# Norm's mean from its rows, opening by row tiles, modulation in quarters, and the values ahead of the root in head 0

## The chip, the cores and the metric

The kernel runs on one core of a Trainium2 chip. The time is device microseconds of one execution. TensorE multiplies (PE in the profile, with its weight loads PEld), VectorE (DVE) and ScalarE (ACT) do the elementwise work, GpSimd (POOL) and SyncE (SP) here mostly issue DMAs. All engines run on their own and meet at semaphores.

## The reference

One step of a two layer diffusion backbone on 128 context and 512 latent tokens (640 columns in five row tiles), 1024 channels. Layer 0 mixes by latent attention with 8 heads, layer 1 by a Conformer convolution; each is followed by a SwiGLU FFN. Each part starts from a root mean square norm with a shift and a scale that a conditioning vector makes:

```python
sh1, sc1, g1, ... = split(silu(cond) @ w_mod[l] + b_mod[l], 6)
h = rms_norm(x, norm_mix[l]) * (1 + sc1) + sh1
# layer 0
q = rms_norm((rms_norm(h @ w_dq) @ w_uq) per head);  kv = h @ w_dkv
k, v = split(rms_norm(kv[:256]) @ w_ukv);  k = rms_norm(concat(k, kv[256:]))
o = softmax(q k^T * scale) v
# layer 1
y = depthwise_conv(glu(h @ w_pw1))
y = silu((y - mean(y)) * rsqrt(mean((y - mean(y))**2) + eps) * ln_g + ln_b) @ w_pw2
```

## The kernel before

The program is written by hand for each engine: every engine has its list of instructions and waits for semaphores. Activations lie with channels on the partitions (eight tiles of 128 channels, `KT`) and tokens along the row. Precision comes from three products for each matmul: a number is split in a high and a low part (`HH` and `HL`, `WH` and `WL`), and `split3` adds high x high, high x low and low x high. PSUM is used as four tiles of two banks, given out in the order of `tile_order()`: the n-th name gets tile n mod 4, and `begin` waits until the tile's last user was read. `filled` waits for a product, `was_read` for the release of its tile.

*Opening.* SyncE loads x (`XROWS`, by rows), the first weights (`RAW`, unit `dkv` 0) and the first 2048 columns of `w_mod`, as two halves of 512 columns of shift and scale each, in 8 loads per half (`MODS`). TensorE turns x into channel order (L805), sums its squares over the channels (L817), and multiplies the modulation's rows (L853), four column groups of 32 at once; ScalarE copies the rows (`MROW`), TensorE turns them (L864), VectorE adds the bias and makes the gains (`first_half`, L1814 and L1819). The sums are turned too (L829), VectorE takes their inverse root and makes diagonals, which TensorE spreads over the partitions (`spread`, L790) and ScalarE copies to `RSTD`. Then `apply` makes, tile by tile, the scaled tile (L1891, VectorE), its high part (L1330, ScalarE) and its low part (L1905, VectorE), and TensorE runs the pair `dkv` 0 and 1 over the eight tiles k0 to k7. Half the modulation's columns serve tiles 0 to 3, the other half tiles 4 to 7; the second half's rows are multiplied inside the pair (`second_half`). `hold_clock` multiplies constants, to keep TensorE at work.

*Head 0.* Keys, queries and values come from the same unit. TensorE turns the values (`v`, L1006), ScalarE copies their high part `VH` and VectorE makes the low part `VL` (L2104). The head's squares are summed to `hsum`, copied to `HROW` (L1463), turned (`hst`), and VectorE makes the root and six diagonals (L2093); their spread is `rk`. The order of tiles is `v`, `hsum`, `hst`, `s` 0, `rk`, so `rk` gets the tile of `v`.

*LayerNorm.* The convolution's eight tiles `Y` are shifted by an estimate of their mean (`SHIFT`), tiles 0 to 5 by DMAs of GpSimd; ScalarE squares them (`LNQ`, L1709), and TensorE sums the squares (L1235) and the tiles (`srow`). The rest of the mean is spread over the partitions by matmuls with ones (`mean_part`, L1242), and leaves as `OFFSET`. ScalarE then makes a low part for a later unit (L1674), loads the table of Silu (L1716) and copies `RSTD`.

## Time and profile before

| | |
|---|---|
| median of 3 runs | 1640.55 us (1639.95 to 1641.98) |
| the profiled run | 1642.74 us, its span 1640.9 us |
| TensorE busy | 1607.8 us, 98% |
| VectorE, ScalarE, GpSimd busy | 56%, 41%, 18% |
| the DMAs | 178.12 MB, mean 109 GB/s |
| mean granted clock of TensorE | 0.993 |

The busy share of TensorE is an average; what counts for a change in one place is which wait ends last there. So the timeline and the waits of that place are read, with the granted clock beside them (1.0 is 2.4 GHz, 0.5 is 1.2 GHz).

### The profile page before, as it was taken

What the parts mean: (1) busy time and instruction counts of PE and PEld (TensorE: products, weight loads), DVE (VectorE), ACT (ScalarE), POOL (GpSimd) and SP (SyncE); (2) the same over time, 40 slices, a digit from 0 to 9 for tenths busy, and PEclk for the clock granted to TensorE, in tenths of its full rate; (3) what the DMA queues carried; (4) which work ended last, traced back from release to release, by engine and by line L of the source; (5) the groups of instructions that cost most, each with busy time, mean ns of one, the idle gap of its engine ahead of it and who ended that gap; (6) DMA issues with size and microseconds to landing.
All of it is one profiled execution on the core that took longest, in us unless ns stands there. A gap on an engine that the chain in (4) does not pass through costs nothing.

```text
span 1640.9 us, 26141 instructions
## 1 busy us (share of the span) xinstructions
PE 1607.8 (98%) x11077; PEld 1558.9 (95%) x11077; DVE 922.3 (56%) x1537; ACT 666.4 (41%) x1002; POOL 287.6 (18%) x344
## 2 busy tenths in 40 slices
PE   7989999999999999999999999999999999999998
PEld 5889889899999999999999999989999999999998
DVE  4646667665776645455367889987742323223232
ACT  3435555553544323342335656674432212221121
POOL 0011111000155423453342022230000000000000
PEclk8999999999999999999999999999999999999999
DMA  9322333132254433443333288873232122222211
GB/s 320 99 66 84 92 99 103 35 116 78 89 162 141 155 112 122 155 133 123 115 115 108 55 180 180 182 138 98 71 94 78 61 77 77 77 77 77 71 59 65
DMA packets 140157, 178.12 MB, mean 109 GB/s; under 512 B 12769, under 2 KB 116905, under 8 KB 139016
## 3 DMA queue, kind: packets, MB, share of 16 engines
q1 hardware_dynamic: 117824, 109.68, 21.0%
q0 software_dynamic: 21888, 66.66, 16.2%
q8 instruction: 88, 1.44, 0.4%
q14 instruction: 29, 0.24, 0.0%
q10 hardware_dynamic: 328, 0.10, 0.0%
HBM read 148.93 MB, written 2.79 MB: 92 GB/s over the span
## 4 chain that ended last, share of the span: by engine, by line
PE 85%; DVE 10%; DMA 2%; ACT 2%; issue 1%; POOL 0%; SPq 0%; DVEq 0%; ACTq 0%; POOLq 0%
PE PS L693 26%; PE PS L695 25%; PE PS L698 25%; DVE YACC L2319 6%; DMA ZACC<-ZTAP 1%; PE PS L763 1%; PE PS L1019 1%; PE PS L790 1%; PE PS L1030 1%; PE PS L982 1%; DMA XROWS<-in_x_sample 1%; DVE GP L2283 0%; PE PS L805 0%; DVE HL L1905 0%; PE PS L963 0%
## 5 line engine op out<-in xcount | busy, mean ns | idle before, releaser
L693 PE MATMUL PS<-HH,WH 128*128 128x320 f32 x1776 | 411.1, 313 | 6.0 <-DVE HL L1905 5.6
L695 PE MATMUL PS<-HL,WH 128*128 128x320 f32 x1776 | 405.5, 310 | 0.0
L698 PE MATMUL PS<-HH,WL 128*128 128x320 f32 x1776 | 404.2, 309 | 0.0
L1756 DVE TENSOR_TENSOR WL<-RAW,WH 128x2048 fp32r<-128x2048 f32 (+2 forms) x87 | 196.4, 2258 | 203.2 <-ACT WH L1294 203.1
L693 PEld LDWEIGHTS PS<-HH,WH 128*128 128x128 f32 x1776 | 295.9, 189 | 10.3 <-issue 6.8
L695 PEld LDWEIGHTS PS<-HL,WH 128*128 128x128 f32 x1776 | 298.6, 189 | 0.0
L698 PEld LDWEIGHTS PS<-HH,WL 128*128 128x128 f32 x1776 | 298.3, 189 | 0.0
L1294 ACT ACTIVATE WH<-RAW 128x2048 fp32r<-128x2048 f32 (+2 forms) x95 | 171.6, 1806 | 111.2 <-PE PS L698 111.2
L1921 DVE SCALAR_TENSOR_TENSOR X<-PS,MODV,X 128x128 f32<-128x128 f32 (+2 forms) x192 | 72.4, 433 | 198.7 <-PE PS L698 198.5
L615 POOL TENSOR_TENSOR BGACC<-BGACC,BGW 128x512 f32<-128x512 f32 x98 | 135.0, 1378 | 194.9 <-ACT BGW L1550 193.8
L693 PE MATMUL PS<-HIDH,WH 128*128 128x320 f32 x704 | 162.3, 312 | 0.7 <-DVE HIDL L2242 0.7
L698 PE MATMUL PS<-HIDH,WL 128*128 128x320 f32 x704 | 160.7, 309 | 0.0
L695 PE MATMUL PS<-HIDL,WH 128*128 128x320 f32 x704 | 160.5, 309 | 0.0
L1550 ACT ACTIVATE BGW<-BGW,SC 128x512 f32<-128x512 f32 x112 | 80.7, 723 | 157.4 <-DVE BGACC L1859 116.4
L2319 DVE SCALAR_TENSOR_TENSOR YACC<-GP,WTAP,YACC 128x655 f32<-128x655 f32 x143 | 128.9, 901 | 5.0
L693 PEld LDWEIGHTS PS<-HIDH,WH 128*128 128x128 f32 x704 | 117.0, 188 | 1.3 <-DVE HIDL L2242 0.9
L698 PEld LDWEIGHTS PS<-HIDH,WL 128*128 128x128 f32 x704 | 117.7, 188 | 0.0
L695 PEld LDWEIGHTS PS<-HIDL,WH 128*128 128x128 f32 x704 | 117.5, 188 | 0.0
L2235 DVE TENSOR_TENSOR TMP<-PS,ACTV 128x640 f32<-128x640 f32 x44 | 36.2, 824 | 133.8 <-PE PS L698 132.8
L1585 ACT ACTIVATE HIDH<-TMP 128x640 fp32r<-128x640 f32 x44 | 32.6, 740 | 181.2 <-DVE TMP L2235 181.2
L1859 DVE SCALAR_TENSOR_TENSOR BGACC<-BGW,SC,BGACC 128x512 f32<-128x512 f32 x98 | 86.4, 882 | 4.8
L1580 ACT ACTIVATE ACTV<-PS 128x640 f32<-128x640 f32 x40 | 28.1, 703 | 130.9 <-PE PS L698 130.9
(340 smaller groups left out, 2285.5 us busy)
## 6 DMA issues: line engine op xcount, KB each, us to landing
BGW<-in_w_mod POOLq DMA_DIRECT2D x112, 256.0 KB, 3.0
RAW<-in_ffn_w_gate SPq DMA_DIRECT2D x22, 1024.0 KB, 5.3
RAW<-in_ffn_w_up SPq DMA_DIRECT2D x22, 1024.0 KB, 5.3
RAW<-in_ffn_w_down SPq DMA_DIRECT2D x16, 1024.0 KB, 5.1
MODA<-in_w_mod POOLq DMA_DIRECT2D x48, 256.0 KB, 3.9
MODS<-in_w_mod SPq DMA_DIRECT2D x16, 512.0 KB, 12.3
RAW<-in_conv_w_pw SPq DMA_DIRECT2D x16, 512.0 KB, 5.1
WL<-RAW POOLq DMA_DIRECT2D x8, 1024.0 KB, 10.1
```

Source lines behind the costliest of these rows:

```text
L615: ins = nc.gpsimd.tensor_tensor(acc, acc, w, ALU.add)
L693: mm(o, wh, xh, start=first, stop=False)
L695: mm(o, wh, xl, start=False, stop=False)
L698: ins = mm(o, wl, xh, start=False, stop=last)
L1294: A(WH[:, u % 2, 0:n], RAW[:, u % 2, 0:n], ACT.Copy).then_inc(hi_done, 1)
L1550: A(w, w, ACT.Copy, scale=SC[:, i % KT, 1:2]).then_inc(sem("bgw_scaled"), 1)
L1585: A(HIDH[:, (a + j) % HID_SLOTS, :], TMP[j][:], ACT.Copy).then_inc(sem("hid_hi"), 1)
L1756: V.tensor_tensor(WL[:, u % 2, 0:n], RAW[:, u % 2, 0:n], WH[:, u % 2, 0:n].bitcast(F32), ALU.subtract).then_inc(lo_done, 1)
L1859: ins = V.scalar_tensor_tensor(out=acc, in0=w, scalar=c, in1=acc, op0=ALU.mult, op1=ALU.add)
L1921: ins = V.scalar_tensor_tensor(out=X[:, m, t:t + b - a], in0=tile2(n)[:, bank, a:b], scalar=g, in1=X[:, m, t:t + b - a], op0=ALU.mult, op1 ...
L2235: V.tensor_tensor(row2(TMP[j][:]), tile2(n)[:, :, 0:HALF], row2(ACTV[j][:]), ALU.mult).then_inc(free_of(n), 1)
L2319: ins = V.scalar_tensor_tensor(out=acc[:], in0=g[:, j:j + RUN], scalar=WTAP[:, i, j:j + 1], in1=ZACC[i % 2][:] if i and j == j0 else acc[: ...
```

## The change

*Opening.* x comes in five loads, one for each row tile, and is turned, copied, squared and summed by row tiles. The sums have 640 columns (`MIXROW`) and are turned in five. The first half of the modulation is loaded in front of the first weights; the second half is loaded, multiplied, copied, turned and read in two quarters of 256 columns. The spread of the root stands in front of the turn of the first half. VectorE's first low part of weights stands behind its first scaled tile, and ScalarE's second copy of them behind its first high part. Four groups of held matmuls are gone.

*Head 0.* On ScalarE `values(0)` stands in front of `sum_rows(0)`, on VectorE in front of `head_norm(0)`.

*LayerNorm.* The mean is spread by two matmuls over the turned sums' rows (`LNROW`), with columns of ones where a row belongs to it (`PAIRS`), behind the transposes; `mean_part` is gone. Tile 6 is squared first. The table is loaded in front of `OFFSET`.

```diff
...
-    o = [("x", k) for k in range(KT)] + ["vec"]
-    o += [("stat", "mix0"), ("turn", "mix0"), ("mrow", 0), ("mods", 0), ("rb", "mix0"), ("mrow", 1), ("mods", 1)]
+    o = [("x", t) for t in range(QT)] + ["vec"]
+    o += [("stat", "mix0"), ("turn", "mix0"), ("mrow", 0), ("rb", "mix0"), ("mods", 0), ("mrow", 1), ("mods", 1)]
...
-    o += ["mu", ("srow", "ln"), ("stat", "ln"), ("turn", "ln"), ("rb", "ln")] + [("pw2", m) for m in range(KT)] + ffn(1)
+    o += [("srow", "ln"), ("stat", "ln"), ("turn", "ln"), "mu", ("rb", "ln")] + [("pw2", m) for m in range(KT)] + ffn(1)
...
-        XSQ = [*SQ, *TMP, *ACTV, SUM, RSTD]
+        XSQ = [sb(f"XSQ{t}", [P, KT, P], R_T[0] + 4096 * t) for t in range(QT)]
+        MIXROW = sb("MIXROW", [P, TOK], R_T[0])
...
-            def load_mods(h):
+            def load_mods(h, part, c0, n):
                 for k in range(KT):
                     w = w_mod[0, k * P:(k + 1) * P, 0:2 * D].rearrange("p (c n) -> p c n", c=2)
-                    sp.dma_start(MODS[h][k][:], w[:, :, h * 512:(h + 1) * 512]).then_inc(mods_landed[h][k], 16)
+                    c = 512 * h + c0
+                    sp.dma_start(MODS[h][k][:, :, c0:c0 + n], w[:, :, c:c + n]).then_inc(mods_landed[part][k], 16)
...
-            sp.dma_start(XROWS[:, 0, :], x_prompt[0]).then_inc(sem("x_landed"), 16)
-            sp.dma_start(XROWS[:, 1:QT, :], x_sample[0].rearrange("(t p) d -> p t d", p=P)).then_inc(sem("x_landed"), 16)
+            sp.dma_start(XROWS[:, 0, :], x_prompt[0]).then_inc(x_landed[0], 16)
+            for t in range(1, QT):
+                sp.dma_start(XROWS[:, t, :], x_sample[0, (t - 1) * P:t * P, :]).then_inc(x_landed[t], 16)
+            load_mods(0, 0, 0, 512)
...
-                    load_mods(0)
-                    load_mods(1)
+                    load_mods(1, 1, 0, 256)
+                    load_mods(1, 2, 256, 256)
...
+            for t in range(QT):
+                ps = begin(("x", t))
+                if t == 0:
                     hold_clock(ps, HOLD)
-                    pe.wait_ge(sem("x_landed"), 32)
-                for t in range(QT):
-                    ins = tr(flat(ps)[:, t * P:(t + 1) * P], XROWS[:, t, k * P:(k + 1) * P], EYE[:])
+                pe.wait_ge(x_landed[t], 16)
+                for k in range(KT):
+                    ins = tr(flat(ps)[:, k * P:(k + 1) * P], XROWS[:, t, k * P:(k + 1) * P], EYE[:])
...
+            for t in range(QT):
+                pe.wait_ge(sem("sq_made"), SQ_BASE["mix0"] + t + 1)
+                for e in range(2):
+                    for g in range(GROUPS):
+                        ins = mm(ps[COLG * g:COLG * (g + 1), t // 4, t % 4 * P:(t % 4 + 1) * P], ONES[:, 0:COLG], XSQ[t][:, 2 * g + e, :],
+                                 start=(e == 0), stop=(e == 1))
+            ins.then_inc(mm_done, 1)
             def turn_sums():
-                hold_clock(ps, HOLD // 4)
                 out = begin(("turn", "mix0"))
                 was_read(pe, ("stat", "mix0"))
-                for i in range(3):
-                    ins = tr(out[:, 0, i * P:(i + 1) * P], HROW[:, i * P:(i + 1) * P], EYE[:])
+                for t in range(QT):
+                    ins = tr(flat(out)[:, t * P:(t + 1) * P], MIXROW[:, t * P:(t + 1) * P], EYE[:])
                 ins.then_inc(mm_done, 1)
-                hold_clock(out, HOLD // 4)
...
+            def later_rows(q):
+                rows = begin(("mrow", 1)) if q == 0 else tile2(("mrow", 1))
+                for k in range(0, KT, 2):
+                    pe.wait_ge(mods_landed[1 + q][k], 16)
+                    pe.wait_ge(mods_landed[1 + q][k + 1], 16)
+                    for g in range(GROUPS):
+                        i = k + g // 2
+                        ins = mm(rows[COLG * g:COLG * (g + 1), q, 0:256], SC[:, i, :], MODS[1][i][:, g % 2, 256 * q:256 * (q + 1)],
+                                 start=(k == 0), stop=(k == KT - 2))
+                ins.then_inc(mm_done if q else sem("part_rows"), 1)
...
+            def turn_later(q):
+                if q == 0:
+                    pe.wait_ge(sem("part_copied"), 1)
+                    turn_rows_of(begin(("mods", 1)), 0, range(2)).then_inc(sem("part_turned"), 1)
+                else:
+                    was_read(pe, ("mrow", 1))
+                    turn_rows_of(tile2(("mods", 1)), 1, range(2, 4)).then_inc(mm_done, 1)
             def second_half(k, j):
                 if (k, j) == (0, 1):
-                    first_rows(1, KT // 2, KT - 2)
-                if (k, j) == (2, 0):
-                    first_rows(1, KT - 2, KT)
-                if (k, j) == (2, 1):
-                    turn_first(1)
+                    later_rows(0)
+                if (k, j) == (3, 1):
+                    later_rows(1)
+            turn_sums()
             pe.wait_ge(sem("sc_ready"), 2)
-            first_rows(0, 0, KT // 2)
-            turn_sums()
-            first_rows(0, KT // 2, KT)
-            turn_first(0)
+            first_rows()
             spread(("rb", "mix0"), diagn, DIAGS["mix0"])
-            first_rows(1, 0, KT // 2)
+            turn_first()
...
+                if k == KT // 2 - 1:
+                    turn_later(0)
                 if k == KT // 2:
+                    turn_later(1)
...
+                    pe.wait_ge(sem("sq_made"), SQ_BASE["ln"] + k + 3)
...
-            mean_part(SEVENS, SHIFT, True, False)
             pe.wait_ge(sem("sq_added"), NORMS["mu"])
-            mean_part(ONES, SUM, False, False).then_inc(mm_done, 1)
             for g in range(GROUPS):
                 mm(means[COLG * g:COLG * (g + 1), 0, 0:3 * P], (ONES, SEVENS)[g // 2][:, 0:COLG], (SUM, SHIFT)[g // 2][:, halves3[g % 2]],
                    start=True, stop=g >= 2)
-            for k in range(0, KT - 2, 2):
-                square_sums(k)
+            square_sums(0)
+            square_sums(2)
             pe.wait_ge(sem("last_shifted"), 1)
             for g in range(2):
                 ins = mm(means[COLG * g:COLG * (g + 1), 0, 0:3 * P], ONES[:, 0:COLG], Y[:, KT - 1, halves3[g]], start=False, stop=True)
             ins.then_inc(mm_done, 1)
+            square_sums(4)
...
-            mean_part(ONES, Y[:, KT - 1, :], False, True).then_inc(sem("mean_whole"), 1)
+            mean = begin("mu")
+            pe.wait_ge(sem("pairs_made"), 2)
+            for i in range(2):
+                ins = mm(mean[:, i, 0:HALF], PAIRS[i][:], LNROW[:, 1, i * COLG * 2:i * COLG * 2 + HALF], start=True, stop=True)
+            ins.then_inc(mm_done, 1)
...
+            for t in range(QT):
+                was_read(act, ("x", t))
+                A(XSQ[t][:], X[:, :, t * P:(t + 1) * P], ACT.Square).then_inc(sem("sq_made"), 1)
...
-            A(HROW[:], tile2(("stat", "mix0"))[:, 0, 0:3 * P], ACT.Copy).then_inc(free_of(("stat", "mix0")), 1)
+            A(MIXROW[:], flat(tile2(("stat", "mix0")))[:, 0:TOK], ACT.Copy).then_inc(free_of(("stat", "mix0")), 1)
+            filled(act, ("mrow", 0))
+            A(MROW[:], tile2(("mrow", 0))[:, 0, :], ACT.Copy).then_inc(free_of(("mrow", 0)), 1)
+            spread_copy(("rb", "mix0"), RSTD, QT)
             act.wait_ge(raw_landed[0], landed[0])
             A(WH[:, 0, 0:UNIT // 2], RAW[:, 0, 0:UNIT // 2], ACT.Copy).then_inc(sem("hi_first"), 1)
-            A(WH[:, 0, UNIT // 2:UNIT], RAW[:, 0, UNIT // 2:UNIT], ACT.Copy).then_inc(hi_done, 1)
-            n_hi[0] += 1
-            def first_row_copy(h):
-                filled(act, ("mrow", h))
-                A(MROW[:], tile2(("mrow", h))[:, 0, :], ACT.Copy).then_inc(free_of(("mrow", h)), 1)
-            first_row_copy(0)
-            spread_copy(("rb", "mix0"), RSTD, QT)
             def first_between(k):
-                if k == KT // 2 - 1:
-                    first_row_copy(1)
+                if k == 0:
+                    A(WH[:, 0, UNIT // 2:UNIT], RAW[:, 0, UNIT // 2:UNIT], ACT.Copy).then_inc(hi_done, 1)
+                    n_hi[0] += 1
+                if k == 2:
+                    act.wait_ge(sem("part_rows"), 1)
+                    A(MROW[:, 0:256], tile2(("mrow", 1))[:, 0, 0:256], ACT.Copy).then_inc(sem("part_copied"), 1)
+                if k == 3:
+                    filled(act, ("mrow", 1))
+                    A(MROW[:, 256:512], tile2(("mrow", 1))[:, 1, 0:256], ACT.Copy).then_inc(free_of(("mrow", 1)), 1)
...
+            values(0)
             sum_rows(0)
-            values(0)
             spread_copy(("rk", 0), RK, NKT)
             for h in range(HEADS):
                 for t in range(QT):
...
                 if i:
                     tap_diagonals(i)
                     conv_out(i - 1)
-            for i in range(KT - 1):
+            for i in (KT - 2, *range(KT - 2)):
                 act.wait_ge(y_shifted[i], 16)
                 A(LNQ[i][:], Y[:, i, :], ACT.Square).then_inc(sem("sq_made"), 1)
             for b, n in ((1, ("srow", "ln")), (0, ("stat", "ln"))):
                 filled(act, n)
                 A(LNROW[:, b, :], tile2(n)[:, 0, 0:3 * P], ACT.Copy).then_inc(free_of(n), 1)
-            act.wait_ge(sem("mean_whole"), 1)
+            A(REC8[:, 0:1], ONES[:, 0:1], ACT.Silu)
...
-            A(LNSS[:, 0:1], ONES[:, 0:1], ACT.Silu)
...
+                if first is not None:
+                    first()
...
+                V.tensor_copy(X[:, :, t * P:(t + 1) * P], flat(tile2(n)).rearrange("p (k c) -> p k c", c=P)).then_inc(free_of(n), 1)
...
-            dve.wait_ge(sem("hi_first"), 1)
-            split_first(0)
-            n_lo[0] += 1
+            def low_first():
+                dve.wait_ge(sem("hi_first"), 1)
+                split_first(0)
+                n_lo[0] += 1
...
-                    first_half(1)
-            first_half(0)
-            apply("mix0", 0, 0, second=between)
+                    dve.wait_ge(sem("part_turned"), 1)
+                    first_part(("mods", 1), 0, 4, 6)
+                if k == KT // 2:
+                    filled(dve, ("mods", 1))
+                    first_part(("mods", 1), 1, 6, 8)
+            filled(dve, ("mods", 0))
+            first_part(("mods", 0), 0, 0, 4)
+            apply("mix0", 0, 0, second=between, first=low_first)
...
             queries(0)
+            values(0)
             head_norm(0)
-            values(0)
             split_units(U[("head", 1)])
             for h in range(HEADS):
                 was_read(dve, ("rk", h))
...
             for s in range(2):
                 link(V.tensor_tensor(GB[:, s, :], MODV[:, 1, s, 16:24], VT2[:, V2["b_pw2"]:V2["b_pw2"] + KT], ALU.mult))
+            for g in range(2):
...
+                rows = EYE[:].rearrange("p (e g c) -> p g c e", e=2, g=2)[:, g, 0:1, :]
+                link(V.tensor_reduce(out=LNSS[:, g:g + 1], in_=rows, op=ALU.add, axis=mybir.AxisListType.X))
+                V.tensor_scalar(PAIRS[g][:], ONES[:], LNSS[:, g:g + 1], None, ALU.mult).then_inc(sem("pairs_made"), 1)
...
```

TensorE in the opening, from the last rows of the first half (`MODS_6`, `MODS_7`) to the first product of the pair (`HH`, `WH`); before:

```order
L853 MATMUL PS<-MODS_6_63,SC 32x512 [waits mods_landed0_7,mods_landed0_6]
L853 MATMUL PS<-MODS_6_63,SC 32x512
L853 MATMUL PS<-MODS_7_64,SC 32x512 x2
L864 MATMUL PS<-PICK_185,MROW 128x4 [waits tile_read3,pick_made,tile_read0]
L864 MATMUL PS<-PICK_185,MROW 128x4 x3
L790 MATMUL PS<-DIAGN,ONES 128x128 [waits diag_ready,tile_read1]
L790 MATMUL PS<-DIAGN,ONES 128x128 [waits diag_ready] x4
L853 MATMUL PS<-MODS_0_65,SC 32x512 [waits mods_landed1_1,mods_landed1_0,tile_read2]
...
L693 MATMUL PS<-HH,WH 128x320 [waits lo_first,h_ready,tile_read1,tile_read0]
```
and now:

```order
L853 MATMUL PS<-MODS_6_63,SC 32x512 [waits mods_landed0_7,mods_landed0_6]
L853 MATMUL PS<-MODS_6_63,SC 32x512
L853 MATMUL PS<-MODS_7_64,SC 32x512 x2
L796 MATMUL PS<-DIAGN,ONES 128x128 [waits diag_ready,tile_read1]
L796 MATMUL PS<-DIAGN,ONES 128x128 [waits diag_ready] x4
L872 MATMUL PS<-PICK_193,MROW 128x4 [waits tile_read0,pick_made,tile_read2]
L872 MATMUL PS<-PICK_193,MROW 128x4 x3
L699 MATMUL PS<-HH,WH 128x320 [waits lo_first,h_ready,tile_read2,tile_read1]
```
The spread (`DIAGN`) moved in front of the turn (`PICK`), and the rows of the second half left the place in front of the pair.

ScalarE inside the pair, from the high part of tile 3 to that of tile 4 (`HH`), with the copy of the modulation's rows (`MROW`); before:

```order
L1330 ACTIVATE HH<-SQ_87,MODV 128x128 [waits t_ready]
L1330 ACTIVATE HH<-SQ_87,MODV 128x512
L1330 ACTIVATE HH<-TMP_89,MODV 128x128 [waits t_ready]
L1330 ACTIVATE HH<-TMP_89,MODV 128x512
L1382 ACTIVATE MROW<-PS 128x512 [waits mm_done]
L1330 ACTIVATE HH<-TMP_90,MODV 128x128 [waits t_ready]
L1330 ACTIVATE HH<-TMP_90,MODV 128x512
```
and now:

```order
L1349 ACTIVATE HH<-SQ_87,MODV 128x128 [waits t_ready]
L1349 ACTIVATE HH<-SQ_87,MODV 128x512
L1406 ACTIVATE MROW<-PS 128x256 [waits part_rows]
L1349 ACTIVATE HH<-TMP_89,MODV 128x128 [waits t_ready]
L1349 ACTIVATE HH<-TMP_89,MODV 128x512
L1409 ACTIVATE MROW<-PS 128x256 [waits mm_done]
L1349 ACTIVATE HH<-TMP_90,MODV 128x128 [waits t_ready]
L1349 ACTIVATE HH<-TMP_90,MODV 128x512
```
One copy became two, the first of them in front of tile 3.

VectorE in head 0, around the root (`RS`) and its diagonals (`DIAGK`); before:

```order
L2040 SCALAR_TENSOR_TENSOR QNL<-PS,GQK,QNH 128x640 [waits qn_hi]
L2088 TENSOR_TENSOR HST<-PS,KPSS 128x12 [waits mm_done]
L2090 SCALAR_TENSOR_TENSOR RS<-HST,MODV 128x12 [waits tile_read1]
...
L2093 TENSOR_SCALAR DIAGK_137<-EYE,RS 128x128 [waits dve_chain]
...
L2094 TENSOR_SCALAR RQ_193<-RS 128x6
L2104 TENSOR_TENSOR VL<-PS,VH 128x768 [waits v_hi,dve_chain]
L1756 TENSOR_TENSOR WL<-RAW,WH 128x1024 [waits hi_done]
```
and now:

```order
L2071 SCALAR_TENSOR_TENSOR QNL<-PS,GQK,QNH 128x640 [waits qn_hi]
L2135 TENSOR_TENSOR VL<-PS,VH 128x768 [waits v_hi]
L2119 TENSOR_TENSOR HST<-PS,KPSS 128x12 [waits mm_done]
L2121 SCALAR_TENSOR_TENSOR RS<-HST,MODV 128x12 [waits tile_read2]
...
L2124 TENSOR_SCALAR DIAGK_143<-EYE,RS 128x128 [waits dve_chain]
...
L2125 TENSOR_SCALAR RQ_201<-RS 128x6
L1775 TENSOR_TENSOR WL<-RAW,WH 128x1024 [waits hi_done,dve_chain]
```
`VL` moved from behind the diagonals to in front of the sums.

## Rows read from the trace of the kernel before

**Rows 1.** The page, part 4: shares of the chain that ended last.
```profile
PE 85%; DVE 10%; DMA 2%; ACT 2%; issue 1%; POOL 0%; SPq 0%; DVEq 0%; ACTq 0%; POOLq 0%
```

**Rows 2.** Timeline of PE, opening (start, us, line, out<-in, count, idle before it and its releaser).
```profile
10.87 7.39 PE L805 MATMUL PS<-EYE,XROWS 128*128 128x128 f32 x40 [3.55 <-DMA XROWS<-in_x_sample]
...
24.06 1.92 PE L853 MATMUL PS<-MODS,SC 128*32 128x512 f32 x16
...
30.51 1.03 PE L864 MATMUL PS<-PICK,MROW 128*128 128x4 f32 x8 [0.81 <-ACT MROW L1382]
31.39 1.36 PE L790 MATMUL PS<-DIAGN,ONES 128*128 128x128 f32 x10
...
36.94 0.70 PE L693 MATMUL PS<-HH,WH 128*128 128x320 f32 x2 [2.34 <-DVE HL L1905]
...
51.03 0.53 PE L693 MATMUL PS<-HH,WH 128*128 128x320 f32 x2 [2.04 <-DVE HL L1905]
...
58.34 0.68 PE L838 MATMUL PS<-EYE,TAPROWS 31*128 31x31 f32 x8
```

**Rows 3.** Loads of the tile MODS, one issued between 13.2 and 13.9 us at the latest.
```profile
L535 SPq DMA_DIRECT2D MODS<-in_w_mod x1: 1300/1300/1300, 13.1 to 13.1; - x1
...
DMA to landing us min/median/max: 12.4/12.4/12.4
```

**Rows 4.** Windows: busy time of PE, PEld, DVE, ACT, POOL, then clock, DMA share, GB/s.
```profile
11.00:13.00 2.00, 2.00 (x10) 2.00 (x11) 0.77 (x1) 0.00 (x0) 0.00 (x0) 0.50 1.08 354
22.00:30.00 8.00, 7.70 (x67) 3.77 (x63) 2.37 (x15) 2.61 (x4) 0.00 (x0) 1.00 1.05 388
37.20:40.50 3.30, 3.30 (x16) 2.91 (x19) 3.30 (x7) 1.91 (x4) 0.00 (x0) 0.50 0.29 82
119.10:125.80 6.70, 4.48 (x19) 4.48 (x20) 3.72 (x12) 0.95 (x2) 0.00 (x0) 0.50 0.26 81
```

**Rows 5.** Timeline of DVE, opening.
```profile
30.36 1.22 DVE L1947 TENSOR_TENSOR WL<-RAW,WH 128x1024 fp32r<-128x1024 f32 x1
31.57 0.24 DVE L1814 TENSOR_TENSOR MODV<-PS,VT 128x8 f32<-128x8 f32 x2
...
33.62 1.94 DVE L1891 SCALAR_TENSOR_TENSOR TMP<-X,GAIN,RSTD 128x128 f32<-128x128 f32 x4 [1.54 <-ACT RSTD L1307]
```

**Rows 6.** Timeline of ACT, opening.
```profile
29.77 0.60 ACT L1382 ACTIVATE MROW<-PS 128x512 f32<-128x512 f32 x1 [3.83 <-PE PS L853]
```

**Rows 7.** Timeline of PE, head 0.
```profile
118.24 0.27 PE L1019 MATMUL PS<-KPL,QP 128*128 128x128 f32 x1
121.32 2.93 PE L790 MATMUL PS<-DIAGK,ONES 128*128 128x128 f32 x12 [2.81 <-DVE VL L2104]
```

**Rows 8.** Timeline of DVE, head 0.
```profile
116.88 0.17 DVE L2088 TENSOR_TENSOR HST<-PS,KPSS 128x12 f32<-128x12 f32 x1 [1.35 <-PE PS L971]
...
118.93 1.27 DVE L2093 TENSOR_SCALAR DIAGK<-EYE,RS 128x128 f32<-128x128 f32 x6
...
120.31 0.96 DVE L2104 TENSOR_TENSOR VL<-PS,VH 128x768 fp32r<-128x768 f32 x1
```

**Rows 9.** Timeline of ACT, head 0.
```profile
115.69 0.49 ACT L1463 ACTIVATE HROW<-PS 128x384 f32<-128x384 f32 x1 [1.08 <-PE PS L963]
116.07 0.81 ACT L1477 ACTIVATE VH<-PS 128x768 fp32r<-128x768 f32 x1
```

**Rows 10.** Timeline of PE, LayerNorm.
```profile
1091.91 2.12 PE L1235 MATMUL PS<-LNQ,ONES 128*32 128x384 f32 x24
...
1096.32 1.24 PE L1242 MATMUL PS<-Y,ONES 128*128 128x320 f32 x4
...
1100.07 1.28 PE L790 MATMUL PS<-DIAGN,ONES 128*128 128x128 f32 x10
```

**Rows 11.** Timeline of ACT, LayerNorm.
```profile
1091.70 1.36 ACT L1709 ACTIVATE LNQ<-Y 128x640 f32<-128x640 f32 x2 [0.92 <-DMA Y<-SHIFT]
...
1100.12 1.28 ACT L1716 ACT_TABLE_LOAD   x1
```

94 lines of the change are left out of this document (39 added, 55 removed).

## The prediction

> **What bounds the kernel now.** I read the page's chain of waits first. TensorE carries 85% of the chain that ended last, VectorE 10% [rows 1], so the kernel is a nearly closed row of matmuls, and time is to be had only where that row is open. Every part of the change lies in one of three such places: the opening, head 0, and the LayerNorm of the convolution. For each I read the timeline of the three engines, and asked what ends each wait of TensorE last.
>
> *Opening.* The transposes of x begin at 10.87, when the one load of the four latent row tiles lands, and end at 18.2; the modulation's rows run until their copy at 29.77 [rows 6], its turn at 30.51, the spread of the root at 31.39, and the first product of the layer starts at 36.94, after 2.34 us of waiting for VectorE. The second half of the modulation's columns is interleaved with that pair of products, which stands once more at 51.03 for 2.04 us and is over at 58.34 [rows 2]. The loads are full work: 388 GB/s from 22 to 30 us, and 354 GB/s while the first weights come in packets of 1 KB [rows 4]. The eighth load of modulation was issued at 13.1 and landed 12.4 us later, at 25.5 [rows 3].
>
> *Head 0.* The root's six diagonals are made from 118.93, but the spread starts at 121.32 and waited 2.81 us for VL, the values' low part, which VectorE makes only at 120.31 [rows 7, 8]: `rk` uses the PSUM tile that `v` held. TensorE's clock is at half from 119.1 to 125.8 [rows 4].
>
> *LayerNorm.* TensorE works through without a gap, but on too much: the sums of squares start at 1091.91 behind four 320 column products, the last piece of the mean at 1096.32, and the spread at 1100.07 [rows 10]. ScalarE loads its table at 1100.12, on the path [rows 11].
>
> **The opening, step by step.** The x tiles now arrive one by one and are copied in five pieces of 1024 columns instead of eight of 640 (VectorE), squared likewise, and summed per row tile. From about 8.5, my guess for when the first tile is turned, five copies at 1.2 (as WL of 1024 columns [rows 5]), a square of as much, the sums and their copy make about 17 us; that has 5 us to spare and isn't the path. What stands last is the modulation. Now its first half (8 loads of 0.52 MB) follows x directly, and the 1 MB of weights comes behind it. From 10.8: 8 x 0.524 MB at 388 GB/s is 10.8 us, so 21.6. The same sum for the kernel before (1.05 MB at 354 GB/s first, 3.0 us) gives 24.6, and it landed at 25.5; I keep that 0.9, so 22.5. Then TensorE: the last two tiles of rows are half of 1.92 (four tiles), to 23.5; the spread 1.3, to 24.8; the turn 1.0, to 25.9, with the copies of 0.60 and the like beside it [rows 2, 6]. VectorE: reading 0.24 + 0.23, to 26.4; then two scaled tiles of about 0.95, WL (now behind the first scaled tile) 1.2, and one low part of 0.95 [rows 5], to 30.5. First product at 30.6 instead of 36.94. The weights' first half must be there by 27.4 for this: landed 25.5, and a copy of 1024 columns is at most 1.2, so 26.7. SyncE issues the same bytes; the 16 loads of quarters have 256 KB each, and `dkv` 2 and the late loads stand behind them as before.
>
> Not all of those 6.3 us stay, because the second half's rows are now all inside the pair. One k step is (58.34 - 51.03) / 4 = 1.8 us at full clock. Before, the first was at half clock, as from 37.2 to 40.5 [rows 4], and cost 3.4. I assume the same now, since TensorE stands idle from 25.9 to 30.6. So: k0 3.4, first quarter's rows 1.9 (as many columns as four half tiles), k1 and k2 3.6, turn 0.5, k3 1.8, second quarter's rows 1.9: 13.1, to 43.7. These rows now lie behind k3, and ScalarE waits for them with its copy **before** the high part of tile 4, so everything queues: copy about 0.45, high part 0.95, low part 0.95, gaps 0.1: k4 at 46.2. VectorE next reads the last gains (0.5), scales and takes the low part of tile 5 (1.9): k5 at 48.6, k6 at 50.5, k7 at 52.3, end of the pair at 54.05 instead of 58.34. **Opening: -4.3 us.** The quarters' loads land, at 354 GB/s (0.524 MB x 4 = 2.1 MB, 5.9 us each), at 31.4 and 37.3, ahead of their use at 34.0 and 41.8; the late loads are queued behind them as before. Bounds: if the clock is full from 30.6 on, 1.6 more is won (-5.9); if it falls already between 22.5 and 26, the spread, rows and turn take about twice as long and the start slips by 2.2 (-2.1). I take the middle, since the kernel before shows one fall here.
>
> One rule speaks against this part. Loads of 512 KB moved 388 GB/s from 22 to 30 us, one in 1.35 us, and the eighth was 12.4 us under way, so about nine overlap [rows 3, 4]; the sum above goes by that. The Trainium skill, "DMA: Bandwidth & Descriptors", section Bandwidth, asks for loads of 1 MiB or more to reach 75% of peak, and gives each load some 2 us of fixed cost. An estimate by its fit, without overlap, is 2.6 us for 256 KB, quarters at 46 and 67 us and a kernel slower than before. The trace disagrees with that at 512 KB, and no run here shows 256 KB; a milder form is a rival below.
>
> **Head 0.** Both moves fill holes. On ScalarE VH (0.81) now precedes HROW, which had 1.08 us of idle time before it [rows 9]; on VectorE VL (0.96) precedes the sums, before which it had 1.35 idle [rows 8]. So neither delays the root: the sums are read at 116.88 as before, and the first diagonal is there at 119.15, when the scores of the context are over (118.5, the last product of rows 7 started 118.24). What is late next is the root itself. Spread: 12 instructions, at full clock 1.55 (ten took 1.28 in the LayerNorm [rows 10]), to 120.7 instead of 121.32 + 2.93 = 124.25: 3.55. Before, TensorE ran at half until 125.8, which cost another 0.8. **Head 0: -4.3 us** if the clock doesn't fall. If it falls at 119 and rises at 122.5, the spread takes 2.9 and the first scores are slowed: -2.8.
>
> **LayerNorm.** Ahead of the squares' sums, 8 matmul instructions of 320 columns go (1.24 us twice, as in the row of 1096.32), and the last piece behind the transposes goes too; two products of 320 columns over the turned row take their place (1.1). The squares now end with tile 5, whose DMA decides: ScalarE's two last squares ran 1091.70 to 1093.06, so tile 5 is squared at 1092.4; TensorE has done the others, and sums 2 x 0.65, to 1093.75. Before, 24 of these instructions ended at 1094.0, and 0.63 for the mean of tile 7 and 0.65 for tiles 6 and 7 made it 1095.3. Everything behind is 1.6 earlier: turn, root, mean (over at 1095.95 instead of 1097.57), held clock, spread over at 1099.7. ScalarE has loaded its table (1.28 + 0.2) while it waited for the mean, and starts the spread's copy at 1099.8 instead of 1101.6, to where the table held it [rows 11]. The new VectorE instructions (two reductions, two of 128x128, about 1 us) fall where it waits for the turned sums. **LayerNorm: -1.7 us**, bounds -1.4 and -2.2. Late next: TensorE's own held clock in front of the spread.
>
> **Sum:** -4.3 - 4.3 - 1.7 = -10.3 us. The profiled run took 1642.74 us (span 1640.9), so its like would be 1632.4; the median of the three runs is 2.2 lower, and gives 1640.55 - 10.3 = 1630.2. Behind the pair TensorE hardly waits until head 0, and all loads there are released by compute, so I let the gain pass.
>
> **Rivals.**
> *The clock falls in the wrong places* (2 in 10). Held matmuls are removed between 18 and 28 us, and TensorE has more gaps there. For it: half clock stands in rows 4 behind each long gap. Against: the modulation's rows are work too. Opening -2.1, head 0 -2.8, LayerNorm -1.7: 1634.0. In the Trainium skill, "TensorE: Matmul & The Clock Gate", Part 1, the throttled state is the default and activity releases it; what is removed here is such activity, and the traces agree that the clock falls behind gaps.
> *The clock holds in the opening* (1.3 in 10): -5.9 - 4.3 - 1.7: 1628.7.
> *Small loads are slow* (0.6 in 10): if a 256 KB load takes as long as one of 512 KB (1.35 us), the quarters land at 36.3 and 47.1; the second rows end 4 us later, the opening gives 0.3, sum 6.3: 1634.3. Against: the 1 KB packets of the weights at 354 GB/s.
> *The change doesn't do what it says in head 0* (0.4 in 10): something else, say QP's moves, holds the spread as long: 1634.5. Against: the scores in front of it were over at 118.5 [rows 7].
> *Slower* (0.3 in 10): the clock stays at half from the spread at 23.5 to the end of the pair. Price: 1.3 + 1.0 of spread and turn, 14.4 of k steps, 3.8 of rows, 1.0 of turns is 21.5 us of work that would take twice as long, less the 1.6 counted and some 3 that hide in waits: +17, so 1647. It decides for slower once the half clock there is over 20 us longer than counted. Against: both falls of rows 4 ended while TensorE worked.
>
> **Numbers.** Forecast 5.4 in 10. Range 1627 to 1635: it takes in all cases but the last and the edges. About 0.2% (3.3 us) is what a measurement of this kernel can tell: faster 0.93, same 0.04, slower 0.03.
>
> **What would show it.** First product of the layer at about 30.6, pair over at 54; a wait of TensorE for low part 4 in front of k4; the spread of head 0 started by 119.3 and waiting for diagonals; the LayerNorm's spread over 1.6 us sooner after the end of the convolution, and ScalarE's copy waiting for TensorE. Wrong if the eighth modulation load lands after 24, if the quarters land later than 34 and 42, or if the gain is lost to half clock.

## The result: 5.8 us faster where 10.3 were forecast

| | before | after |
|---|---|---|
| median of 15 runs | 1641.76 us (1639.24 to 1644.20) | 1636.00 us (1632.11 to 1639.13) |
| ratio | | 0.9968 (0.9960 to 0.9976) |
| profiled run, its span | 1642.74, 1640.9 us | 1635.48, 1633.7 us |

The sign was right, the size was not: 1636.0 lies above the range of 1627 to 1635. The two profiles differ by 7.2 us, but 1.4 of that is an end of the profiled run of before that no other one has: from the last transpose to the end of the span it took 6.7 us, in the thirteen other profiles of this study 5.2 to 5.3. Until then after is 5.83 us ahead, which is what the medians say too. The starts of the same work, one trace against the other:

| place | before | after | gain so far | forecast |
|---|---|---|---|---|
| first product | 36.94 | 30.41 | 6.53 | 6.3 |
| pair over | 58.34 | 54.22 | 4.12 | 4.3 |
| values' transposes, head 0 | 113.02 | 108.90 | 4.12 | 4.3 |
| `kn` 1, behind head 0's scores | 130.75 | 124.11 | 6.64 | 8.6 |
| last matmul of the convolution | 1088.85 | 1083.03 | 5.82 | 8.6 |
| first product behind the LayerNorm | 1105.76 | 1099.93 | 5.83 | 10.3 |

So three terms fell short: head 0 by 1.8 us, the way from there to the convolution's end by 0.8, the LayerNorm by 1.7. The rows of after that answer to [rows 2] (timeline of PE, opening: start, us, line, out<-in, count, idle before it and its releaser):

```profile
7.42 4.63 PE L811 MATMUL PS<-EYE,XROWS 128*128 128x128 f32 x40
...
22.52 1.06 PE L853 MATMUL PS<-MODS,SC 128*32 128x512 f32 x8 [1.65 <-DMA MODS<-in_w_mod]
23.52 1.38 PE L796 MATMUL PS<-DIAGN,ONES 128*128 128x128 f32 x10
...
30.41 0.87 PE L699 MATMUL PS<-HH,WH 128*128 128x320 f32 x2 [4.72 <-DVE HL L1930]
...
46.38 0.53 PE L699 MATMUL PS<-HH,WH 128*128 128x320 f32 x2 [1.50 <-DVE HL L1930]
...
54.22 0.68 PE L840 MATMUL PS<-EYE,TAPROWS 31*128 31x31 f32 x8
```

The eighth load of the modulation ends TensorE's wait at 22.52 (22.5 in the forecast), k4 waits for low part 4 until 46.38 (46.2), and the pair is over at 54.22 (54.05). Head 0, against [rows 7]:

```profile
115.24 2.06 PE L796 MATMUL PS<-DIAGK,ONES 128*128 128x128 f32 x12 [0.88 <-DVE DIAGK L2124]
...
124.11 0.51 PE L699 MATMUL PS<-CKH,WH 128*128 128x384 f32 x2
```

The spread no longer waits for VL but for the diagonals, as foreseen. It takes 2.06 us, not 1.55, because the clock falls inside it. Windows of after (us, busy time of PE, PEld, DVE, ACT, POOL, granted clock, DMA share, GB/s):

```profile
27.60:34.20 6.60, 3.79 (x16) 3.37 (x20) 6.37 (x13) 3.71 (x7) 0.00 (x0) 0.50 1.10 348
116.40:119.50 3.10, 3.10 (x14) 3.10 (x13) 1.48 (x4) 1.40 (x3) 0.00 (x0) 0.50 0.23 53
```

The first row holds the loads of the quarters, 256 KB each: 348 GB/s, so small loads are not slow, and that rival falls; TensorE didn't wait for either quarter (rows multiplied from 33.88 and 41.83, forecast 34.0 and 41.8). The Trainium skill, "DMA: Bandwidth & Descriptors", section Bandwidth, asks for 1 MiB or more per load to reach 75% of peak; this trace shows no such need for loads that overlap like these (512 KB moved 388 GB/s). The 2 us of fixed cost that the prediction puts under the same section stand in the Trainium skill under "Anatomy of one DMA" on that page, for loads that GpSimd issues; these were issued by SyncE. The LayerNorm of after, PE and then ACT, against [rows 10, 11]:

```profile
1085.46 0.85 PE L1257 MATMUL PS<-LNQ,ONES 128*32 128x384 f32 x8 [0.69 <-ACT LNQ L1728]
...
1088.11 1.50 PE L1257 MATMUL PS<-LNQ,ONES 128*32 128x384 f32 x16 [1.17 <-ACT LNQ L1728]
...
1094.36 1.28 PE L796 MATMUL PS<-DIAGN,ONES 128*128 128x128 f32 x10
```
```profile
1084.67 0.74 ACT L1728 ACTIVATE LNQ<-Y 128x640 f32<-128x640 f32 x1 [3.01 <-DMA Y<-SHIFT]
1085.75 0.74 ACT L1728 ACTIVATE LNQ<-Y 128x640 f32<-128x640 f32 x1 [0.34 <-DMA Y<-SHIFT]
1087.33 0.74 ACT L1728 ACTIVATE LNQ<-Y 128x640 f32<-128x640 f32 x1 [0.83 <-DMA Y<-SHIFT]
...
1090.18 1.28 ACT L1732 ACT_TABLE_LOAD   x1
```

All edits are there: no early mean, the table ahead of `OFFSET`. But TensorE, which had no gap here in before, now stands twice for the squares, and ScalarE for 3.01 us for tile 3, whose DMA landed late. From the issue of the first shift's DMA (1079.21 in before, 1073.41 in after) to the square of tile 5, the last that a DMA shifts, it is 12.49 us in before (1091.70) and 13.92 in after. TensorE's gain of 1.4 went into that wait. The six DMAs of the shifts, each from its own issue to its landing (before, then after):

```profile
DMA to landing us min/median/max: 3.7/6.9/9.8
```
```profile
DMA to landing us min/median/max: 3.7/8.0/11.2
```

Counted from the first issue, they land at 3.71, 5.51, 7.42, 9.16, 10.82 and 12.47 us in before, and at 3.70, 5.55, 7.50, 11.24, 12.32 and 13.89 in after: the first three are on time, the fourth is 2.1 late.

Why did the DMAs take longer? A window of after at their end; then the queues' packets, MB and share from the first shift's DMA to the last one's end (1073.4 to 1087); then, from the page, parts 1 and 3, the counts of the whole run:

```profile
1085.60:1086.90 1.30, 1.30 (x12) 0.25 (x7) 1.20 (x5) 0.74 (x1) 0.00 (x0) 1.00 0.06 12
```
```profile
q0 software_dynamic: 969, 2.20, 92.2%
q8 instruction: 1, 0.02, 0.4%
```
```profile
PE 1599.7 (98%) x11123; PEld 1553.6 (95%) x11123; DVE 922.9 (56%) x1541; ACT 666.2 (41%) x1000; POOL 287.6 (18%) x344
...
q8 instruction: 88, 1.44, 0.4%
```

A DMA share of 0.06 over 1.3 us is one engine of sixteen. The packets, sampled every 0.25 us, say the same: from 7 to 11.75 us behind the first issue 16 to 20 of them are in flight, and from 12.25 to 13.5 us exactly one, where before has none. The queue of instructions moved 88 packets in 1.44 MB, so 16 KB each, for 22246 instructions of TensorE (matmuls and weight loads), about 253 a packet. They are TensorE's: between one packet and the next lie 255 to 258 of its instructions in the median, in all fourteen traces. The one of these fetches in the second fence started at 1082.57, 9.2 us behind the first shift's DMA, when the fourth DMA was next to land. In before they lay 4.0 us ahead of it and 17.2 behind. That made theory F (the texts below call it theory A): the change adds about 112 instructions of TensorE ahead of the convolution (14938 of them stand ahead of the first shift's DMA, 14825 in before), so each fetch comes at an earlier place in the program. One now falls among the shifts' DMAs, where it holds up one of the sixteen engines that each of them needs.

### The profile page after: what moved, and what is told of

It is laid out like the page before. It is cut to its first block, busy times and chain, and to the rows that moved or that the text cites. A ratio compares the mean times of both kernels' runs of the same rounds, so it can differ in the third digit from the quotient of the medians.

```text
span 1633.7 us, 26252 instructions
## 1 busy us (share of the span) xinstructions
PE 1599.7 (98%) x11123; PEld 1553.6 (95%) x11123; DVE 922.9 (56%) x1541; ACT 666.2 (41%) x1000; POOL 287.6 (18%) x344
## 3 DMA queue, kind: packets, MB, share of 16 engines
q0 software_dynamic: 21888, 66.66, 16.4%
q8 instruction: 88, 1.44, 0.4%
## 4 chain that ended last, share of the span: by engine, by line
PE 83%; DVE 9%; DMA 4%; ACT 2%; issue 1%; SPq 1%; POOL 0%; DVEq 0%; ACTq 0%; POOLq 0%
PE PS L699 26%; PE PS L701 25%; PE PS L704 25%; DVE YACC L2350 4%; DMA ZACC<-ZTAP 2%; PE PS L769 1%; PE PS L1041 1%; PE PS L796 1%; PE PS L1052 1%; DMA MODS<-in_w_mod 1%; DMA Y<-SHIFT 1%; PE PS L1004 1%; DVE GP L2314 0%; DVE HL L1930 0%; PE PS L985 0%
```

## The experiments

Twelve runs, one of them after again. Medians, with those of the kernel before from the same comparison:

| | us | before | ratio |
|---|---|---|---|
| e1 LayerNorm alone | 1638.94 | 1641.14 | 0.9991 (0.9982 to 1.0000) |
| e2 head 0 alone | 1637.60 | 1641.14 | 0.9982 (0.9972 to 0.9992) |
| e3 after, held opening | 1633.78 | 1641.14 | 0.9954 (0.9942 to 0.9966) |
| e4 after, both held | 1630.22 | 1641.14 | 0.9935 (0.9923 to 0.9947) |
| e5 opening alone | 1639.37 | 1641.41 | 0.9985 (0.9976 to 0.9993) |
| e6 after again | 1634.46 | 1641.41 | 0.9955 (0.9943 to 0.9968) |
| e7 e4, fetch back | 1640.51 | 1641.41 | 0.9990 (0.9982 to 0.9999) |
| e8 e4, rows early | 1629.45 | 1641.41 | 0.9924 (0.9912 to 0.9936) |
| e9 after, fetch away | 1639.94 | 1640.67 | 0.9992 (0.9983 to 1.0000) |
| e10 before, fetch into | 1647.67 | 1640.67 | 1.0039 (1.0026 to 1.0051) |
| e11 e4, old head 0 | 1634.31 | 1640.67 | 0.9955 (0.9943 to 0.9967) |
| e12 e8, last head held | 1627.50 | 1640.67 | 0.9917 (0.9904 to 0.9930) |

What their traces show, in the second table. *Pair*: when the pair is over; for e7, e9 and e10 less the work inserted behind it. *Head 0*: from the values' transposes to `kn` 1, with the half clock in it. *Fetch*: those next to the first shift's DMA, from its issue. *Tile 5*: from that issue to its square. *LN*: from the last convolution matmul to the first product behind the LayerNorm.

| | pair | head 0 | half clock | fetch | tile 5 | LN |
|---|---|---|---|---|---|---|
| before | 58.34 | 17.73 | 6.8 | -4.0, +17.2 | 12.49 | 16.91 |
| e1 | 55.74 | 17.65 | 6.8 | -3.9, +16.6 | 12.50 | 15.49 |
| e2 | 57.26 | 15.04 | 3.4 | -4.0, +17.2 | 12.50 | 16.91 |
| e10 | 57.5 | 18.13 | 6.8 | **+9.7** | 13.67 | 17.42 |
| e5 | 54.27 | 18.41 | 6.8 | **+9.1** | 13.86 | 17.65 |
| after | 54.22 | 15.21 | 3.4 | **+9.2** | 13.92 | 16.90 |
| e6 | 54.19 | 15.19 | 3.4 | **+8.5** | 13.44 | 16.46 |
| e9 | 55.7 | 13.64 | 0 | -4.3, +16.4 | 12.49 | 15.48 |
| e3 | 53.51 | 16.12 | 6.8 | +0.4, +19.5 | 12.49 | 15.48 |
| e4 | 52.50 | 13.62 | 0 | -3.5, +16.5 | 12.50 | 15.48 |
| e7 | 52.4 | 14.01 | 0 | **+11.9** | 14.28 | 18.55 |
| e8 | 50.54 | 13.62 | 0 | -3.5, +16.5 | 12.48 | 15.53 |
| e11 | 53.52 | 17.12 | 3.4 | -4.1, +14.3 | 12.48 | 15.47 |
| e12 | 51.09 | 13.63 | 0 | -5.2, +14.5 | 12.48 | 14.69 |

**e1, the LayerNorm alone.** The hunks of `mu`, `mean_part`, `PAIRS`, the order of the squares and the table, on the kernel before:

```diff
-            mean_part(SEVENS, SHIFT, True, False)
...
+                ins = mm(mean[:, i, 0:HALF], PAIRS[i][:], LNROW[:, 1, i * COLG * 2:i * COLG * 2 + HALF], start=True, stop=True)
```

> The kernel before with the LayerNorm part of the change alone. Theory A (the place of an instruction fetch decides): TensorE's instructions up to here are those of before, so the 16 KB fetch that fell at 1075.16 in before, ahead of the shifts' DMAs (issued from 1079.21), stays there, all sixteen DMA engines end together, tile 5 is squared about 3.4 us after the last convolution matmul as before, and the part is worth 1.4 to 1.7 us: the first product behind the LayerNorm starts 15.2 us after the last convolution matmul instead of 16.8, time -1.5. Theory B (the sums of squares wait for tile 5 wherever the fetch is, and the part is worth nothing): interval between the two unchanged within 0.3 us, time within 0.3 us of before.

16.91 became 15.49: -1.42, in the forecast's bounds (-1.4 to -2.2). Theory A, and the part as such is sound. (The 3.4 us "of before" in this text are those of tile 6, squared last there; tile 5 is at 2.85.) PE and ACT of e1:

```profile
1088.81 1.50 PE L1236 MATMUL PS<-LNQ,ONES 128*32 128x384 f32 x16 [0.59 <-ACT LNQ L1707]
```
```profile
1088.02 0.74 ACT L1707 ACTIVATE LNQ<-Y 128x640 f32<-128x640 f32 x1 [0.91 <-DMA Y<-SHIFT]
```
TensorE waits once for the squares, 0.59 us, where after has 0.69 and 1.17.

**e2, head 0 alone.**

```diff
+            values(0)
             sum_rows(0)
-            values(0)
```
and on VectorE `values(0)` likewise ahead of `head_norm(0)`.

> The kernel before with the move of the values in head 0 alone. Theory A (the gain is cut by a clock that falls in front of the spread, as in the profiled run of after): the start of kn(1), 130.75 in before, comes 2.5 to 2.8 us earlier, half clock from about 119 to 122.5. Theory B (the forecast: the clock doesn't fall in front of the spread): 4.3 us earlier. Rival C: the opening's change is what made head 0 faster: within 0.3 us of before. The LayerNorm is that of before.

Theory A: 17.73 became 15.04, -2.69, with half clock from 117.9 to 121.3. The spread waits for the diagonals and then takes nearly twice 1.55 us (PE of e2):

```profile
118.28 2.90 PE L790 MATMUL PS<-DIAGK,ONES 128*128 128x128 f32 x12 [0.86 <-DVE DIAGK L2093]
```

**e3, after with the opening held.** `hold_clock` multiplies 128 columns of constants; a step is 4 instructions of TensorE, 0.24 us at full clock.

```diff
             turn_first()
+            hold_clock(tile2(("mods", 0)), 18)
```

> After, with 18 steps of held matmuls (72 instructions of TensorE) between the turn of the first half of the modulation and the first product, where TensorE stands idle for 4.72 us. Theory A (the clock of the first k steps costs 1.6 us, and each 256 instructions of TensorE bring one fetch of 16 KB): granted clock 1.0 from 27.6 to 34.4, pair over about 1.6 us before 54.22; the fetch of 1082.57 comes about 5.9 us earlier, at 1076 to 1077, still among the shifts' DMAs (1073.4 to 1087), so tile 5 is squared again 4 us or more behind the convolution and the LayerNorm gives nothing. Rival B (the second half of the modulation ends late whatever the clock): pair over at 54.2 within 0.4.

Half right. The clock is 1.0 from 27.4 to 34.3, but in the profiled run it fell from 44.8 to 48.2 instead, behind the waits at k4, and the pair won 0.7, not 1.6. The fetch came 8.7 us earlier against the shifts' DMAs instead of 5.9, 0.4 us behind the first, and did no harm: it made the first of the six land 0.5 us late (4.17), the third was on time again (7.38), and the LayerNorm took 15.48, against my number. The place of a fetch can be told from the count of instructions only within some 4 us.

**e4, opening and head 0 held.**

```diff
+                    if k > 2:
+                        hold_clock(rows, 4)
                     pe.wait_ge(mods_landed[0][k], 16)
...
+            hold_clock(tile2(("mods", 0)), 18)
...
+                if h == 0:
+                    hold_clock(ps, 3)
                 was_read(pe, ("hsum", h))
...
+                if h == 0:
+                    hold_clock(tile2(("hst", 0)), 4)
                 head_ready(h)
...
+                        hold_clock(tile2(("s", 0, 0)), 3)
                         key_spread(0)
```

> After, with the same 18 steps, 4 steps in each of the last two waits of the modulation's rows, and 10 steps in the three waits of TensorE in head 0: 36 steps, 144 instructions of TensorE. Theory A: clock 1.0 through opening and head 0, opening -1.6, head 0 -1.8 against after; the fetch of 1082.57 comes 11.8 us earlier, at about 1070.8, ahead of the shifts' DMAs, tile 5 is squared 3.4 us or less behind the last convolution matmul, and the LayerNorm gives 1.4 to 1.7: sum -4.8 to -5.1, about 1631. Rival B (fetches have nothing to do with tile 5): the LayerNorm as in after, sum -3.4. Rival C (held matmuls don't raise the clock there): -1.5 or nothing.

Theory A throughout. Windows of e4, then PE:

```profile
25.50:30.40 4.90, 4.31 (x38) 4.14 (x38) 4.60 (x12) 4.06 (x7) 0.00 (x0) 1.00 1.10 350
...
108.00:121.00 13.00, 12.65 (x95) 11.10 (x95) 10.62 (x38) 5.66 (x12) 1.14 (x3) 1.00 0.35 93
```
```profile
44.67 0.53 PE L699 MATMUL PS<-HH,WH 128*128 128x320 f32 x2 [1.50 <-DVE HL L1938]
...
52.50 0.68 PE L840 MATMUL PS<-EYE,TAPROWS 31*128 31x31 f32 x8
...
113.53 1.57 PE L796 MATMUL PS<-DIAGK,ONES 128*128 128x128 f32 x12
```

Pair over 1.7 us before after's (the forecast's bound said 1.6), head 0 in 13.62 us, LayerNorm in 15.48. It is 10.9 us under before, where after is 5.8 (e6: 7.0). Of that difference the opening gives 1.7 us and head 0 1.6, both by the clock, and 1.0 to 1.4 is the fetch, which the held steps moved away. Its five runs lie within 1.3 us, where after's fifteen spread over 7.0. After's time goes partly with the clock, which differs from run to run: its three fastest runs (1632.1 to 1632.7) had a mean granted clock of 0.996 or 0.997, its three slowest (1638.6 to 1639.1) 0.993 to 0.995. In e2 it is plainer: the three fastest 0.998 at 1634.7 to 1635.0, the three slowest 0.992 or 0.993 at 1641.5 to 1641.6. The Trainium skill, "TensorE: Matmul & The Clock Gate", Part 1, has activity release the throttled state; by that rule the gaps that the change opened had to be filled, and these traces agree.

**e5, the opening alone.**

```diff
-            for k in range(KT):
-                ps = begin(("x", k))
...
+            for t in range(QT):
+                ps = begin(("x", t))
```
and all other hunks of the opening, on the kernel before.

> The kernel before with the opening part of the change alone. The openings of before profiled so far ended the pair at 58.34, 55.74 (e1) and 57.26 (e2), by where the clock fell. Theory A: the pair is over at 54.2 as in after, give or take 0.7; the opening adds about 112 instructions of TensorE, so the fetch lies among the shifts' DMAs as in after, tile 5 is squared late (over 4.2 us behind the last convolution matmul instead of 3.5), and the old LayerNorm takes 18.2 us from there to its first product instead of 16.9: in time -3 + 1.4, about -1.6 to -2.5 against before. Theory B (no such fetch effect): 16.9 and -3 to -4.1. Head 0 takes 17.7 from the values' transposes to kn(1), as before.

-2.0 (by the ratio -2.5), theory A: pair over at 54.27, a fetch at +9.1, and the old LayerNorm lost 0.74 us to it (I had said 1.3).

**e6, after again**, no edit.

> After, unchanged: does what its profile showed repeat? Theory A (the place of the fetch is the program's): a fetch at 1080 to 1085, tile 5 squared 4 us or more behind the last convolution matmul, 16.9 us from there to the first product behind the LayerNorm; pair over at 54.2, first product at 30.4. Theory B (it was that execution's chance): LayerNorm 15.5. Time 1636 in both, B up to 1.4 less in its profiled run.

A again: fetch at +8.5, LayerNorm 16.46. The loss is the program's, its size (1.4 or 1.0) the execution's.

**e7, a fetch brought back into e4.**

```diff
+            hold_clock(tile2(("mods", 1)), 22)
             late_rows()
```

> The kernel of e4 with 22 more steps of held matmuls (88 instructions of TensorE, 5.2 us of work on the path) between the pair and the late rows. Theory A (where the fetch falls decides): it comes back among the shifts' DMAs, as in after about at the end of the convolution (0.5 us before the last convolution matmul starts), tile 5 is squared over 4.2 us behind that matmul, and the LayerNorm takes 16.9 instead of 15.5 us: time 5.2 + 1.4 = 6.6 over e4, 1636.8. Theory B (the fetch has nothing to do with it): 15.5 us, 5.2 over e4, 1635.4.

The fetch is back and tile 5 late by 1.8 us. Only 1.0 of this is the fetch's: the first five DMAs land 0.8 to 1.0 late already (from 4.49 on, e4 from 3.70), ahead of the fetch at 11.9, and why stays open. The time is 10.3 over e4, 3.7 more than I said: TensorE, standing 1.0 us for VectorE's shift of a tile of `Y` and 1.2 for the squares, lost its clock from 1091.7 to 1095.2, so the LayerNorm took 18.55 us, and in head 7, where it fell too, went 1.4. So the size of the loss here is not a test of the fetch alone.

**e8, the second quarter's rows one k step earlier.**

```diff
-                if (k, j) == (3, 1):
+                if (k, j) == (2, 1):
+                    turn_later(0)
                     later_rows(1)
...
-                if k == KT // 2 - 1:
-                    turn_later(0)
```

> The kernel of e4 with the second quarter's rows one k step earlier (behind k2 instead of k3, and the first quarter's turn in front of them). Theory A (what holds k4 is ScalarE's copy of the rows and the high and low part of tile 4 queued behind it): the wait of 0.50 for the copy and that of 1.50 for low part 4 go, k4 at 42.7 instead of 44.67, pair over at 50.3 to 50.8 instead of 52.50, time -1.7 to -2.2 against e4, 1628.0 to 1628.5. Rival B: the second quarter's loads are not there at 38.2, TensorE waits for them and the gain is under 0.7. The rest as in e4.

In the trace as said (PE of e8): no wait for the loads, and the wait at k4 went from 1.50 to 0.32 us.

```profile
38.15 1.93 PE L867 MATMUL PS<-MODS,SC 128*32 128x256 f32 x32
...
42.70 0.53 PE L699 MATMUL PS<-HH,WH 128*128 128x320 f32 x2 [0.32 <-DVE HL L1937]
...
50.54 0.68 PE L840 MATMUL PS<-EYE,TAPROWS 31*128 31x31 f32 x8
```

The pair is over 1.96 us earlier. The median shows 0.8 of it (1.0 by the distances to before). In the profile 1.4 went again at 337, where the clock fell in head 7; e12 looks at that.

**e9 and e10, the fetch moved alone.** The line of e7 with 30 steps in after, and with 25 in before. Nothing else in the program differs. The held steps also lie on TensorE's path and keep it at work there, so that the clock fell at other places than in after (e9 in the opening, not in head 0); what tests theory F is the stretch from the first shift's issue to the LayerNorm's end, more than the time.

> After, with 30 steps of held matmuls (120 instructions of TensorE, 7.1 us of work on the path) between the pair and the late rows; opening, head 0 and LayerNorm as in after. In after a fetch fell 9.2 us (and in e6 8.5 us) behind the first of the shifts' DMAs, and the LayerNorm took 16.90 (16.46) us. Theory A (where the fetch falls decides): it now falls within 1.5 us of the first shift's DMA or ahead of it, the next 20 us later behind them all, tile 5 is squared 2.9 us behind the last convolution matmul, and the LayerNorm takes 15.5 us. Theory B (after's LayerNorm is slow by itself): 16.5 to 16.9. Time: A 7.1 - 1.2 = 5.9 over after, B 7.1.

> The kernel before, with 25 steps of held matmuls (100 instructions, 5.9 us of work) between the pair and the late rows. Its fetches fell 4.0 us ahead of the first shift's DMA and 17.2 us behind it. Theory A: the second comes to about 9 us behind it, among the shifts' DMAs; tile 5 is squared over 4.2 us behind the last convolution matmul instead of 3.5, and the old LayerNorm takes 17.6 to 18.3 us instead of 16.91; the GpSimd chains of the convolution lose some tenths more. Time 5.9 + 0.7 to 1.4 over before. Theory B: 16.9 us and 5.9.

Both as theory A has them. By the distances to before e9 is 5.0 us over after and 6.2 over e6, for 7.1 us of added work (said: 5.9); its LayerNorm takes 15.48. e10 is 7.0 over before (said: 6.6 to 7.3). From the first shift's issue to the end of the DMAs e9 has no packet of the instruction queue, e10 has one (queues of e9, then of e10). Behind them, windows and ACT of e10:

```profile
q0 software_dynamic: 869, 1.97, 91.0%
```
```profile
q0 software_dynamic: 993, 2.26, 94.2%
q8 instruction: 1, 0.02, 0.4%
```
```profile
1095.00:1097.30 2.30, 2.30 (x10) 1.43 (x8) 2.16 (x5) 0.47 (x1) 0.00 (x0) 1.00 1.07 193
1097.40:1099.40 2.00, 2.00 (x25) 0.63 (x24) 1.41 (x4) 1.14 (x2) 0.00 (x0) 1.00 0.06 10
```
```profile
1097.42 0.74 ACT L1710 ACTIVATE LNQ<-Y 128x640 f32<-128x640 f32 x1 [1.94 <-DMA Y<-SHIFT]
1099.00 1.36 ACT L1710 ACTIVATE LNQ<-Y 128x640 f32<-128x640 f32 x2 [0.84 <-DMA Y<-SHIFT]
```

The share is 1.07 until 1097.3 and then 0.06: again one engine of sixteen. The DMAs of e10 land 0.2 to 0.3 us late up to the fourth (9.38) and 1.2 from the fifth on (12.07), which was next to land when the fetch started at 9.7. The old LayerNorm lost 0.51 us by it, a little less than I had said (0.7 to 1.4).

e9 also shows what the forecast had as the opening's lower bound: the clock fell from 22.7, in the last rows and the spread, the first product starts at 31.98 and the pair is over at 55.7, -2.6 against before (bound -2.1; PE of e9):

```profile
22.48 1.74 PE L853 MATMUL PS<-MODS,SC 128*32 128x512 f32 x8 [1.65 <-DMA MODS<-in_w_mod]
24.15 2.32 PE L796 MATMUL PS<-DIAGN,ONES 128*128 128x128 f32 x10
...
31.98 0.87 PE L699 MATMUL PS<-HH,WH 128*128 128x320 f32 x2 [4.73 <-DVE HL L1931]
```

**e11, e4 with the old head 0**: the diff of e2 taken back from e4.

> The kernel of e4 with the order of head 0 as in before (values behind the sums' copy and behind the root); its held matmuls stay. It parts the order from the clock. Theory A (the order is worth what the forecast said, about 3, and the clock the rest): from the values' transposes to kn(1) 15.8 to 17.3 us instead of 13.62, TensorE waiting over 1.5 us for VL in front of the spread; time 2.2 to 3.7 over e4. Theory B (held matmuls alone bring the gain): 14.0 us or less, time as e4. The LayerNorm is that of e4, 15.5 us.

17.12 against 13.62, and 4.1 us in the median (4.6 by the distances to before): theory A, though over the 2.2 to 3.7 that I had said; 1.0 of it is the opening, where the clock fell from 44.6. Held matmuls don't bring the gain without the order, since the wait for VL is still there and the clock falls behind it (PE of e11):

```profile
116.51 2.93 PE L796 MATMUL PS<-DIAGK,ONES 128*128 128x128 f32 x12 [2.08 <-DVE VL L2143]
```

**e12, head 7 held in e8.**

```diff
...
                 ps = begin(("pt", h, t))
+                if (h, t) == (HEADS - 1, 3):
+                    hold_clock(ps, 4)
...
                 ps = begin(("o", h, g))
+                if (h, g) == (HEADS - 1, 0):
+                    hold_clock(ps, 2)
```

> The kernel of e8 with 4 steps of held matmuls in the wait of 0.86 us in front of the turn of tile 3 in head 7 and 2 steps in the wait in front of its first weighted values. In some profiles (before at 344, after at 338, e8 at 334, not e1, e2 and e4) the clock falls there once, and what lies behind is 1.3 us later. Theory A: no half clock around 334, 1.3 us won there in that profile, the median 0.5 to 1.0 under e8 (1629.45). Rival B: the 6 steps only cost 0.5 us, and the clock falls or not as before: 1629.5 to 1630.

Windows of e8 and of e12:

```profile
334.30:337.40 3.10, 3.10 (x17) 3.10 (x16) 3.10 (x6) 0.50 (x2) 0.00 (x0) 0.50 0.00 0
```
```profile
326.00:340.00 14.00, 12.90 (x100) 12.21 (x99) 13.01 (x29) 12.63 (x25) 1.63 (x3) 1.00 0.32 99
```

Theory A: 1.35 us won there, the median 2.0 under e8's (1.2 by the distances to before), more than the 0.5 to 1.0 that I had said. At 1627.5 it is the fastest of all, 13.2 us under before, and 6.2 to 7.4 under after by the distances to before. Its LayerNorm is at 14.69 because its last convolution matmul comes later against the shifts (10.45 us behind the first, 9.6 in before); why stays open.

## Why the forecast was right, and where it failed

*Opening, -4.3: right in the pair of profiles (-4.12), too high as an average.* Every step of it was met within 0.2 us but for the clock: I counted one fall, in k0, and it stood at half from 27.4 to 34.3, in front of the first product as well, where TensorE stood anyway. The step that failed is the base: I took the profiled opening of before as typical. It had half clock for 6.8 us from 9.9 on [rows 4 show a part], where e1 and e2, with the same opening, had 3.4 us; they start the first product at 35.8, not 36.94, and over the four openings of that kind the pair ends at 58.3, 57.3, 55.7 and 57.5, 57.2 on average, against 54.2, 54.2, 54.3 and 55.7 in the new one. That is -2.6. e5's -2.0 to -2.5 agrees, with a small loss to the fetch in it.

*Head 0, -4.3: the mechanism right, the term mis-sized.* The spread waits for the diagonals, started at 115.24 (119.36 on before's time axis, forecast 119.15). But "if the clock doesn't fall" was the wrong one of my two values: it fell in head 0 in before, after, e1 to e3, e5, e6, e10 and e11, and stayed up only in e9 and where it was held with the new order. The term was the lower bound, -2.8: measured -2.52 and -2.69 (e2). Kept high, it is -4.1 (e4), all that I had taken. The prediction gives no reason for the higher value, and the waits of TensorE ahead of the spread were there to read: 0.68 and 0.93 us in the trace of before (0.68, 0.89 and 0.88 in after), and the forecast itself has the third, for the diagonals.

*LayerNorm, -1.7: right alone (-1.42), nothing in place (0 in after, -0.45 in e6).* The failed step is the sentence that the squares end with tile 5 "whose DMA decides", at 1092.4, taken over from before. Nothing in the diff touches those DMAs. The opening's added instructions moved the fetches, and tile 5 came 1.4 us later. e1, e6, e9 and e10 show both sides of it, in both LayerNorms.

*"Behind the pair I let the gain pass": wrong by 0.8 us.* Between head 0 and the convolution's end after wins 0.4 us at about 185 and loses 0.7 at 245 and 0.5 at 1058, each at a DMA of GpSimd (PEld and DVE of after):

```profile
238.37 0.14 PEld L1004 LDWEIGHTS PS<-MODA,SC 128*32 128x32 f32 x2 [0.46 <-DMA MODA<-in_w_mod]
```
```profile
1052.89 0.90 DVE L2350 SCALAR_TENSOR_TENSOR YACC<-GP,WTAP,ZACC 128x655 f32<-128x655 f32 x1 [0.47 <-DMA ZACC<-ZTAP]
```

Before has neither wait. Steps of this size (0.3 to 1.2 us, either way) stand between any two of these traces, e1 and e2 too, mostly at DMAs of GpSimd. That a fetch makes some of them is possible and was not tested; they stay open, and so does the cause of this term.

*The sum.* Opening -2.6, head 0 -2.8 (mean of after and e6 against that of before, e1, e5 and e10 is -2.8), LayerNorm -0.2, the rest +0.3 to +0.8: -4.8 to -5.3, and -5.8 measured in one comparison, -7.0 in the other. The rival "the clock falls in the wrong places" (1634.0) was the nearest in kind: its head 0, -2.8, is what happened. Its opening is not, since the first product of after didn't slip, and it kept the LayerNorm's -1.7, with no fetch in it. That three rivals lay at 1634.0 to 1634.5, near the measured 1636.0, is no credit to them: "small loads" and "head 0 does nothing" fell by the traces, and so did "slower" and, for after, "the clock holds in the opening".

## What to carry to other kernels

One profile is one draw: where a clock that falls decides the terms, look at what it costs in several executions before taking a difference from one, and fill a gap that an edit opens with held matmuls in the same step; here that was worth 3 to 4 us more, beside the edit's 6 to 7 (e4, without the fetch's part). An edit that adds instructions to an engine moves that engine's instruction fetches through the whole program. A wait for a chain of DMAs on all sixteen engines, far away from the edit, has then to be looked at again.

## What the hardware showed that I had not expected

An instruction fetch of 16 KB costs the DMAs around it more than its share. In nine profiles without a fetch more than 0.4 us into the shifts' six DMAs, tile 5 came 12.48 to 12.50 us behind the first issue, the same to 0.02 us. In the five with one, 8.5 to 11.9 us in, it came after 13.44 to 14.28, 1.0 to 1.8 more, while the packet itself is 16 KB beside 2 MB and took 0.9 to 1.0 us. In each of the five the DMA that was next to land when the fetch started lands 1.0 to 2.0 us later against the one ahead of it than in before. With what was late before the fetch taken off (0.8 in e7, 0.2 in e10), 0.9 to 1.4 us stay. At the end one packet is in flight, on one engine. The Trainium skill, "DMA: Bandwidth & Descriptors", section Queues, rings and completion order, has each DMA engine take turns between the queues that have work for it. The traces agree in so far as one engine alone falls behind.

The clock falls at a gap in some executions and not in others: at head 7, behind waits of 0.86, 0.68 and 0.40 us, it fell in eight of the thirteen profiles without held steps there (1.1 us in before against e1, 1.4 in e8 against e4), and not in e12, the one with them.
